# First layers: queries and keys, and the PLE gate, each in seven products instead of eight

## The reference

```python
for i in range(DEPTH):                       # DEPTH = 2, 256 tokens, D = 1024
    h = rms_norm(x, norm_g[i])
    proj = h @ w_in[i]                       # 1024 x 4096: eight column blocks of 512
    rq, rk, rv, rz, mq, mk, mv, mz = jnp.split(proj, cuts, axis=-1)
    r_out = retention(rotary(heads(rq, RET_HEADS), pos), rotary(heads(rk, RET_HEADS), pos),
                      heads(rv, RET_HEADS), ret_norm_g[i])
    r_out = jax.nn.silu(rz.astype(f32)) * r_out
    q_m = rms_norm(heads(mq, MOBA_HEADS), q_norm_g[i])
    k_m = rms_norm(heads(mk, MOBA_HEADS), k_norm_g[i])
    m_out = moba(q_m, k_m, heads(mv, MOBA_HEADS), rel_bias)
    m_out = jax.nn.silu(mz.astype(f32)) * m_out
    y = jnp.concatenate([r_out, m_out], axis=-1).astype(x.dtype) @ w_out[i]
    x = x + y
    gate = jax.nn.sigmoid((rms_norm(x) @ w_ple_gate[i]).astype(f32))     # 1024 x 1024
    e = rms_norm(p[i] @ w_ple[i], ple_norm_g[i]).astype(f32)
    x = x + (gate * e).astype(x.dtype)
```

## Time and profile before

| what | value |
|---|---|
| runs | 1550.19, 1550.38, 1552.74 us (median 1550.38) |
| the profiled execution | 1548.3 us, its span 1546.5 us |
| PE busy over the span | 1313.7 us (85%) |
| DVE, ACT, POOL busy | 438.0, 277.0, 225.3 us |
| first two layers, on PE | from 1 us to 368 us |
| chain that ended last, by engine | PE 27%, DMA 23%, SP's queue 20% |

### The profile page before, as it was taken

How to read it: one execution, slowest core, us unless ns; L and a number is a source line. 1 busy time by engine, 2 the same in 40 slices (tenths; PEclk the granted TensorE clock), 3 DMA queues, 4 the chain that set the end, 5 groups by cost and what they waited for, 6 DMA issues and landing times.

```text
span 1546.5 us, 22261 instructions
## 1 busy us (share of the span) xinstructions
PE 1313.7 (85%) x9360; PEld 705.1 (46%) x9360; DVE 438.0 (28%) x884; ACT 277.0 (18%) x541; POOL 225.3 (15%) x138
## 2 busy tenths in 40 slices
PE   9999999999999999667767767999999676776776
PEld 5754466546868554223323223656544232232332
DVE  2654343642845531110100101286411010010011
ACT  2142310423422220300000000215211110101010
POOL 0673026330000008790000000000000000000000
PEclk9999999999999999988998899999999898899789
DMA  9922732246530699999999999945799999999997
GB/s 373 351 100 109 262 128 100 98 167 249 212 137 31 224 427 417 428 427 428 430 428 428 428 428 429 398 165 213 281 429 426 424 431 426 426 429 427 427 427 315
DMA packets 45445, 498.21 MB, mean 322 GB/s; under 512 B 6721, under 2 KB 9537, under 8 KB 13121
## 3 DMA queue, kind: packets, MB, share of 16 engines
q1 hardware_dynamic: 45376, 497.22, 78.3%
HBM read 495.11 MB, written 2.10 MB: 321 GB/s over the span
## 4 chain that ended last, share of the span: by engine, by line
PE 27%; DMA 23%; SPq 20%; DVE 3%; issue 1%; ACT 1%; DVEq 0%; ACTq 0%
DMA weight_ring<-in_moe_weights 21%; SPq L2833 19%; PE banks L3047 5%; PE banks L331 3%; DMA x_normed<-in_moe_weights 3%; PE banks L3058 2%; PE banks L1683 2%; PE banks L1876 2%; PE banks L3022 2%; PE banks L2479 2%; PE banks L2388 1%; PE banks L3092 1%; PE banks L1225 1%; PE banks L1808 1%; PE banks L1814 1%
## 5 line engine op out<-in xcount | busy, mean ns | idle before, releaser
L3047 PE MATMUL banks<-weight_ring,arena 128*32 128x512 f32 x1472 | 217.5, 723 | 123.0 <-DMA weight_ring<-in_moe_weights 121.4
L2965 DVE TENSOR_TENSOR arena<-arena,banks 64x512 f32<-64x512 f32 x32 | 22.1, 690 | 654.9 <-ACT arena L2888 654.9
L3047 PEld LDWEIGHTS banks<-weight_ring,arena 128*32 128x32 f32 x1472 | 45.6, 121 | 278.6 <-issue 139.6
L3022 PE MATMUL banks<-arena,x 128*128 128x64 f32 x960 | 115.4, 281 | 0.0
L3022 PEld LDWEIGHTS banks<-arena,x 128*128 128x128 f32 x960 | 115.2, 200 | 0.0
L331 PE MATMUL banks<-weight_ring,hT 128*128 128x512 f32 x256 | 112.5, 594 | 0.2 <-issue 0.2
L3058 PE MATMUL banks<-weight_ring,arena 128*32 128x512 f32 x728 | 91.2, 627 | 22.0 <-DMA weight_ring<-in_moe_weights 10.0
L2888 ACT ACTIVATE arena<-banks 64x512 f32<-64x512 f32 x32 | 18.9, 592 | 488.9 <-PE banks L3047 488.9
L3092 PE MATMUL banks<-arena 64*128 64x512 f32 x240 | 59.6, 615 | 21.0 <-ACT arena L2894 21.0
L331 PEld LDWEIGHTS banks<-weight_ring,hT 128*128 128x128 f32 x256 | 47.9, 190 | 57.1 <-issue 56.8
L3047 PE MATMUL banks<-arena 128*32 128x512 f32 x352 | 56.7, 666 | 13.4 <-DMA arena<-in_moe_weights 13.4
(11 more groups left out here) (543 smaller groups left out, 1807.6 us busy)
## 6 DMA issues: line engine op xcount, KB each, us to landing
weight_ring<-in_moe_weights SPq DMA_DIRECT2D x137, 2048.0 KB, 26.8
weight_ring<-in_ring_weights SPq DMA_DIRECT2D x35, 2048.0 KB, 10.8
arena<-in_moe_weights SPq DMA_DIRECT2D x18, 2048.0 KB, 43.9
spare_weights<-in_moe_weights SPq DMA_DIRECT2D x10, 2048.0 KB, 44.5
mix<-in_moe_weights SPq DMA_DIRECT2D x9, 2048.0 KB, 47.5
arena<-in_moe_weights SPq DMA_DIRECT2D x17, 1024.0 KB, 43.0
x_normed<-in_moe_weights SPq DMA_DIRECT2D x9, 1024.0 KB, 40.4
hT<-in_moe_weights SPq DMA_DIRECT2D x9, 1024.0 KB, 46.0
```

Of the source, the lines that this page charges most:

```text
L3022: ins = pe.matmul((b_x, b_dn)[k // 4][:, k % 4 * 2 * CAP:(k % 4 + 1) * 2 * CAP], g.x[:, tt, k * P:(k + 1) * P], Pr[:, tt, :], start=(tt == ...
L3047: ins = pe.matmul(b_gu[q:q + CAP, :], xg[:, 2 * quarter + k, e * CAP:(e + 1) * CAP], up_w(where, quarter, e)[:, which, k, :], start=(quart ...
```

## The change

1. **Queries and keys in seven.** Chunks 2 and 3 become a pair too. `qk_product` runs seven products Q1, Q2, Q6, Q5, Q3, Q7, Q4, each of four heads by one token tile: 16 matmuls of 128x128, whose stationary operand is a block of weights. Together they take 112 matmuls of 128x128 instead of 64 of 128x256. They go to six banks (`QK_BANK`); DVE puts them together (`qk_combine`, seven instructions), with the results left in the banks, and rotates each block (four heads by one tile) as it is formed, with the half products written to bank 3.
2. **The sums of inputs** S1 to S4 of the layer's input move from POOL to DVE (`layer_inputs`).
3. **The gate in seven.** `w_ple_gate`'s two chunks become a pair, loaded ahead of `w_ple`. `gate_product` runs G1 to G7, DVE forms their inputs (`ple_inputs`) and combines them (`ple_combine`), the sigmoid is taken from the combined quarter, and the quarters come in the order 0, 1, 3, 2. A product of a pair waits until both of its chunks have landed.
4. **POOL** has eight more differences of weights in each layer. `sum1` and `sum2` of the two new pairs are cut into four instructions of 128x512 (`by_row`); `sum3` and `sum4` are not.
5. **Order.** In the first layer PE runs Q1 ahead of the small matmuls for the tables, in the second P1 goes between Q1 and the transposes. All the products of queries and keys stand before P6, P2 and the scores. O6 comes ahead of the first quarter of `p @ w_ple`. Chunk slots are freed by other products (`free_when`). The four transposed tiles of the next norm stand inside G4 and inside a projection of the next layer. The scaling of the rotary tables comes after both head norms.

The diff, cut to what the text speaks of:

```diff
@@ ring_chunks
+        out += [("w_ple_gate", l, c * 512, c * 512 + 512, KT) for c in range(2)]
         out += [("w_ple", l, 0, D, 2)]
-        out += [("w_ple_gate", l, c * 512, c * 512 + 512, KT) for c in range(2)]
...
@@ first_layers
-        for i, when in enumerate((q.prj(3), q.prj(4), q.prj(6), q.prj(8), q.prj(15), q.prj(15), q.prj(22), q.prj(22),
-                                  q.y(7), q.y(5), q.e(4), q.g(3), q.g(4))):
+        for i, when in enumerate((q.prj(3), q.prj(4), q.qk(7), q.qk(5), q.prj(11), q.prj(11), q.prj(18), q.prj(18),
+                                  q.y(7), q.y(5), q.g(7), q.g(5), q.e(4))):
...
+    GATE_BANK = {G1: 5, G2: 5, G6: 0, G5: 4, G3: 1, G7: 0, G4: 1}
+    QK_BANK = {Q1: 5, Q2: 5, Q6: 6, Q5: 7, Q3: 0, Q7: 1, Q4: 2}
+    QK_TURN = 3
...
+            def layer_inputs(q):
+                dve.wait_ge(*q.qkt(4))
+                TT_(S1, A21, A22, ALU.add).then_inc(q.ai.sem, 1)
+                dve.wait_ge(*q.ai(1))
+                TT_(S2, S1, A11, ALU.subtract).then_inc(q.ai.sem, 1)
+                dve.wait_ge(*q.ai(2))
+                TT_(S4, A12, S2, ALU.subtract).then_inc(q.ai.sem, 1)
+                TT_(S3, A11, A21, ALU.subtract).then_inc(q.ai.sem, 1)
...
+            def rotated(q, l, turn, key, tt, product):
+                heads = lambda ap: ap.rearrange("p (h t) -> p h t", h=4)
+                src, t1, t2 = heads(ps[QK_BANK[product]]), heads(tmp[:, 0:HALF]), heads(ps[QK_TURN])
...
+                layer_inputs(q)
...
+                dve.wait_ge(*q.qkT(4))
+                qk_combine(q, C11)
+                dve.wait_ge(*q.qc(1))
+                rotated(q, l, 1, 0, 0, Q2)
+                qk_combine(q, U2)
+                qk_combine(q, U4)
+                qk_combine(q, C12)
+                dve.wait_ge(*q.qc(1 + C12))
+                rotated(q, l, 2, 1, 0, Q3)
+                qk_combine(q, U3)
+                qk_combine(q, C22)
+                dve.wait_ge(*q.qc(1 + C22))
+                rotated(q, l, 3, 1, 1, Q7)
+                qk_combine(q, C21)
+                dve.wait_ge(*q.qc(1 + C21))
+                rotated(q, l, 4, 0, 1, Q4)
+                combine(q, 0, U2)
...
@@ gpsimd
+            def by_row(which, out, left, right):
+                if which not in (QK, PLE_SUMS):
+                    return sub(out, left, right)
+                for k in range(HT):
+                    ins = sub(out[:, k, :], left[:, k, :], right[:, k, :])
+                return ins
...
+                sum1(l, QK)
+                sum2(l, QK, *([was.y(O6), was.t4(OUT + 1)] if l else []))
+                sum3(l, QK, q.qk(Q1))
+                sum4(l, QK, q.qk(Q2))
+                sum1(l, V)
+                sum2(l, V, *([was.g(G6), was.t4(PLE_SUMS + 1)] if l else []))
+                sum3(l, V, done(q, 0, P1))
...
+                pool.wait_ge(*done(q, 1, P3))
+                sum1(l, PLE_SUMS)
+                sum2(l, PLE_SUMS, done(q, 1, P6), q.t4(G + 1))
...
+                pool.wait_ge(*q.ga(4))
+                sum3(l, PLE_SUMS, q.g(G1))
+                sum4(l, PLE_SUMS, q.g(G2))
@@ tensor
...
+                for h in range(4):
+                    hs = slice(h * P, (h + 1) * P)
+                    for k in range(HT):
+                        ins = pe.matmul(ps[QK_BANK[n]][:, hs], right[:, k, hs], left[:, k, :], start=(k == 0), stop=(k == HT - 1))
...
+                else:
+                    qk_product(l, Q1)
+                    product(l, 0, P1)
+                    qk_transposes(l)
+                    qk_product(l, Q2)
+                for n_ in (Q6, Q5, Q3, Q7, Q4):
+                    qk_product(l, n_)
+                product(l, 0, P6)
+                product(l, 0, P2)
...
-                natural(l, 11, g.hT, 2, GATE_BANK[2], q.g.sem)
-                n_in[l + 1].transposes(pe, 0)
-                natural(l, 12, g.hT, 3, GATE_BANK[3], q.g.sem)
+                for n_ in (G6, G5, G3, G7):
+                    gate_product(l, n_)
+                gate_product(l, G4, lambda: n_in[l + 1].transposes(pe, 0))
```

324 lines of the change are left out of this document (207 added, 117 removed).

## The result

The changed kernel took 1553.84 us (median of 13 runs, 1547.57 to 1559.63), the kernel before 1551.57 us (13 runs beside them): a ratio of 1.0024, 95% interval 1.0013 to 1.0034, so slower by some 3.7 us (the two medians lie 2.3 us apart). Two executions in a slower state, one of the kernel before at 1570.10 us and one of experiment 8 at 1570.45 us with its profile, are left out of every ratio and every row. A second comparison of the same two kernels gave 1.0014 (0.9998 to 1.0030), some 2.2 us, with an interval that just reaches "no change". The forecast was 1548.4 us with a range up to 1553.0: wrong in size and in sign. The profiled execution has a span of 1551.1 us against 1546.5.

The account below looks back on a forecast made before the run. PE was taken to bound the kernel up to 368 us, so its savings move everything behind. The terms 2.7 - 2.45 + 0 - 2.25 = -2.0 us gave 1550.4 - 2.0 = 1548.4 us, range 1543.5 to 1553.0.

Parts of the forecast that it names:

- The matmuls: Queries and keys, each layer: seven products at 3.57 us each take 24.99 instead of 27.74, 2.75 us saved.
- The gates: Gate in both layers: seven products save 3.43 us, PE waits 0.8; net -2.45 and -2.25 us.
- O6's loss: Each layer: O6 waits 0.2 us for its input sum, as `p @ w_ple` no longer stands ahead of it.
- the forecast's first premise: Stretch ahead of 368 us: what PE saves there moves everything behind it, the experts' weight transfers included, by as much.
- The second front: Second layer's start: the head norm's scaling waits for `sum3`, 2.7 us lost against 2.75 saved, 0 in sum.
- The first front: First layer up to P5: waits for chunk 3 and for S2 (Q6 3.8 us late) make it +2.7 us.
- I let S3 follow S4 at once (58.5): First layer's sums on DVE: S3 runs straight behind S4, with no further wait for a POOL difference.
- the +4.8 course: First layer: if POOL gets in between S4 and S3, DVE starts 4 us later; +4.8 in place of +2.7.
- the margin of 0.2 us: First layer: DVE wants S1 at 45.7, 0.2 us after POOL's last short difference starts at 45.5.
- rival 3: First layer: S1 comes behind `sum3`'s start, each sum waits 4.53 us; front +8.0, P5 at 85.4, kernel 1553.7 us; chance 0.15.
- rival 4: First layer: PE's clock falls to 1.2 GHz in the 3.8 us wait, adding 3.8 us; kernel 1552.2 us; chance 0.08.
- a gap that I had priced at 1.6 us: First layer, ahead of Q1: PE is free at 33.39, chunk 3 lands at 34.99, so 1.6 us are lost.

Follow-up runs that it names:

- experiment 8: Changed kernel with the tables' small matmuls ahead of Q1 again, Q1 still waiting for both chunks; run twice: 1550.34 us (0.9997) and 1550.02 us (0.9996 of the kernel before).
- experiment 5: The changed kernel once more, without an edit, for a second profile: 1551.78 us, ratio 1.0014 to the kernel before.
- e1: Changed kernel with Q1, Q2, P1 and P2 waiting only for the one chunk they read: 1544.56 us, ratio 0.9956 to the kernel before.

## Why the prediction was wrong

*The matmuls* were right: L1130 takes 3.57 a product at clock 1.00, and 2.75 us a layer are saved.

*The gates* were right and a little low: 2.98 us gained from O4's end to the projection behind the first gate ((187.30 - 154.65) less (193.13 - 163.46)), forecast 2.65 before O6's loss. PE waits 0.15 there and not 0.8. From P5 to the next front each layer gains 2.57, forecast 2.45 and 2.25. But of these 5 us the runs of the gate alone keep 2.8: that everything behind the first layers moves by as much, the forecast's first premise, does not show in their time, and why stays open.

*The second front* was right: 2.38 us of idle time, 5.41 us for the scaling, 0 in sum.

*The first front* failed: +2.7 forecast, +8.4 in the profile and +4.15 in the other course. "I let S3 follow S4 at once (58.5), since DVE doesn't wait between them" is the step that is wrong in every execution: S3 took 5.0 in all seven profiles in which the sums stand on DVE and the differences are uncut, also where, as in e1, nobody waited for it. S3 and not Q6 then sets the front: the scores start 17.0 us behind S3's end in six of these profiles, all but e1. That gives the +4.8 course named as an unknown (4.15 measured), and with it the whole change stands near -0.6 us: no change. The chunk 5 that P1 waits for (0.59) was left out. And the margin of 0.2 us, by which S1 was said to come too late for the last short instruction, lay within the rounding of the sum: eight times 1.27 is 10.16 and was taken as 10, which moves that instruction's start from 45.7, when S1 is wanted, to 45.5. That S1 took 1.37 in experiment 5, near the 1.8 forecast, was partly luck.

*The rest* is the clock. The forecast held the port's race (rival 3) and the clock (rival 4) for separate mishaps of 0.15 and 0.08. In the first profile they are one mechanism: a gap that I had priced at 1.6 us (2.62 here, since PE came earlier) drops the clock, Q1 takes 1.7 us more, S1 comes behind `sum3`, and every sum waits. The long wait drops the clock again, but that costs nothing there. It leads to 85.8 us, where rival 3 had said 85.4 (and 3.3 us over the kernel before). "If ... the transposes end 1.1 later" was its condition; the clock fulfilled it.

How the 13 runs divide between the two courses is not shown. The one of 85.8 us gives the 3.4 us late start of the even layer. The other alone would leave it 0.9 early, so that the 3.7 and 2.2 us of the two comparisons need either many executions of the first kind or losses behind the first layers; the part of the gates' gain that is missing from their time is of the second kind.

## What to carry to other kernels

A helper that waits for all operands of a pair puts the last landing ahead of the first product: let each instruction wait only for what it reads (here 6 to 10 us in the profiles and 0.6 to 0.7% of the time by the ratios, for one condition on two products). Where a short DVE instruction with two SBUF inputs shares a stretch with POOL, cut POOL's instructions to its length; moved work is priced by the longest instruction on the other side, once for every instruction moved. Follow the moved work to its last instruction too: the forecast priced the wait of the first consumer (Q6), and the stretch was set by the last sum (S3). And where a schedule has margins of tenths of a microsecond, ask which common event uses up several of them at once: the branches are not independent.
